# Softmax steps ahead of the weight split, and two gates behind the copy of turned probabilities

## The reference

```python
# first block, per layer
q = rmsnorm(d_q.reshape(b, s, DIFF_HEADS, 2, DIFF_HALF_DIM), diff_q_norm_g[l])
k = rmsnorm(d_k.reshape(b, s, DIFF_HEADS, 2, DIFF_HALF_DIM), diff_k_norm_g[l])
...
p = jax.nn.softmax(sc, axis=-1)                       # two maps for each head
o = einsum(p, v); o_d = o[:, :, 0] - lam * o[:, :, 1]
y_d = rmsnorm(o_d) * (1 - lam_init) * jax.nn.silu(d_g)
...
y_m = memory_attention(mq, mk, mv) * jax.nn.silu(m_g)
...
# second block: 16 heads, window 128, each with a sink in its softmax
m = jnp.maximum(jnp.max(s, axis=-1, keepdims=True), sink)
p = jnp.exp(s - m)
denom = jnp.sum(p, axis=-1, keepdims=True) + jnp.exp(sink - m)
```

## Time and profile before

| what | value |
|---|---|
| median of 3 runs | 2598.99 us |
| lowest, highest run | 2596.06, 2602.8 us |
| span of the profiled execution | 2596.0 us |
| PE busy | 2547.3 us (98% of the span) |
| PE weight loads busy | 2175.1 us (84%) |
| DVE busy | 1939.5 us (75%) |
| ACT busy | 1300.1 us (50%) |
| mean granted TensorE clock | 0.995 |
| DMA | 556.64 MB, mean 214 GB/s |

### The profile page before, as it was taken

How to read it: one execution, slowest core, us unless ns; L and a number is a source line. 1 busy time by engine, 2 the same in 40 slices (tenths; PEclk the granted TensorE clock), 3 DMA queues, 4 the chain that set the end, 5 groups by cost and what they waited for, 6 DMA issues and landing times.

```text
span 2596.0 us, 35319 instructions
## 1 busy us (share of the span) xinstructions
PE 2547.3 (98%) x13936; PEld 2175.1 (84%) x13936; DVE 1939.5 (75%) x2769; ACT 1300.1 (50%) x1758; POOL 10.8 (0%) x62
## 2 busy tenths in 40 slices
PE   7999999999999999999999999999999999999998
PEld 6888888888888887888788888888888888888886
DVE  6877766887777687676667787887788887788855
ACT  7544555554455555454444554544644443444443
POOL 0000000000000010000000000000000000000000
PEclk9999999999999999999999999999999999999999
DMA  8687554778754466755567788888476668976764
GB/s 271 219 299 244 160 154 143 228 258 286 242 158 152 149 214 218 235 171 154 153 190 222 231 277 277 270 282 272 143 197 189 188 208 307 284 203 196 201 194 140
DMA packets 526519, 556.64 MB, mean 214 GB/s; under 512 B 17409, under 2 KB 453762, under 8 KB 526226
## 3 DMA queue, kind: packets, MB, share of 16 engines
q1 hardware_dynamic: 526354, 554.38, 68.4%
HBM read 552.22 MB, written 2.10 MB: 214 GB/s over the span
## 4 chain that ended last, share of the span: by engine, by line
PE 88%; DVE 7%; ACT 3%; issue 1%; DMA 0%; DVEq 0%; SPq 0%; ACTq 0%
PE ACC L468 43%; PE ACC L473 21%; PE ACC L415 6%; PE ACC L417 6%; PE ACC L416 6%; DVE WL L549 2%; PE OU L1268 1%; ACT WH L540 1%; PE SC L1235 1%; PE SC L1247 1%; ACT PROB L1293 1%; PE SC L1276 1%; DVE XH L1138 0%; DVE XH L1146 0%; DVE PROB L1352 0%
## 5 line engine op out<-in xcount | busy, mean ns | idle before, releaser
L468 PE MATMUL ACC<-XH,WH 128*128 128x512 f32 x5296 | 1692.3, 401 | 21.2 <-DVE XH L1146 15.3
L540 ACT ACTIVATE WH<-RAW 128x1024 fp32r<-128x1024 f32 (+1 forms) x852 | 897.9, 1057 | 1166.5 <-PE ACC L473 836.1
L549 DVE TENSOR_TENSOR WL<-RAW,WH 128x1024 fp32r<-128x1024 f32 (+1 forms) x852 | 1032.6, 1220 | 568.5 <-ACT WH L540 567.0
L473 PEld LDWEIGHTS ACC<-XH,WL 128*128 128x128 f32 x5296 | 998.7, 189 | 236.6
L473 PE MATMUL ACC<-XH,WL 128*128 128x256 f32 x5296 | 1044.2, 279 | 0.0
L468 PEld LDWEIGHTS ACC<-XH,WH 128*128 128x128 f32 x5296 | 814.4, 189 | 41.2 <-issue 18.5
L1932 DVE SCALAR_TENSOR_TENSOR RAWMOD<-RAWMOD,CSILU 128x1024 f32<-128x1024 f32 x192 | 233.8, 1218 | 1.0 <-DMA RAWMOD<-in_w_mod_t 0.7
L415 PE MATMUL ACC<-WH,XH 128*128 128x512 f32 x384 | 151.9, 396 | 3.6 <-DVE WL L549 3.6
L416 PE MATMUL ACC<-WL,XH 128*128 128x512 f32 x384 | 149.6, 390 | 0.0
L417 PE MATMUL ACC<-WH,XH 128*128 128x512 f32 x384 | 149.5, 389 | 0.0
L415 PE MATMUL ACC<-WH,AH 128*128 128x512 f32 x352 | 137.3, 390 | 0.0
(11 more groups left out here) (287 smaller groups left out, 1438.0 us busy)
## 6 DMA issues: line engine op xcount, KB each, us to landing
RAW<-in_w_in SPq DMA_DIRECT2D x408, 512.0 KB, 4.5
RAWMOD<-in_w_mod_t SPq DMA_DIRECT2D x192, 512.0 KB, 4.9
RAW<-in_w_up SPq DMA_DIRECT2D x176, 512.0 KB, 4.7
RAW<-in_w_out SPq DMA_DIRECT2D x96, 512.0 KB, 5.4
RAW<-in_w_down SPq DMA_DIRECT2D x88, 512.0 KB, 5.0
RAW<-in_w_mem_kv SPq DMA_DIRECT2D x32, 512.0 KB, 5.8
RAW<-in_w_branch_gla SPq DMA_DIRECT2D x32, 512.0 KB, 5.1
RAW<-in_w_branch_attn SPq DMA_DIRECT2D x16, 512.0 KB, 5.2
```

The lines of the kernel that those rows point to most:

```text
L468: return pe.matmul(bank, k.WH[:, w % RING, kc, cols], x, start=tile == 0, stop=False)
L473: return pe.matmul(bank[:, 0:T], k.WL[:, w % RING, kc, cols], x[:, 0:T], start=False, stop=tile == tiles - 1)
L540: act.activation(k.WH[:, slot, :, 0:width], k.RAW[:, r % RAWS, :, 0:width], ACT.Copy).then_inc(k.hi_ready, 1)
L549: dve.tensor_tensor(k.WL[:, slot, :, 0:width], k.RAW[:, k.plan.unit_load[unit] % RAWS, :, 0:width], k.WH[:, slot, :, 0:width].bitcast(F32) ...
```

## The change

Nothing is added or removed; steps change place on ACT and DVE. Two new functions take the softmax steps out of `act_beside` and `dve_beside` and are called ahead of the split: `dve_softmax` (maxima and scaling) and `act_softmax` (exponentials). `dve_next_squares` at w = 7 is also called ahead of the split. In the first mem turn of each layer the two gates with their table loads go from w = 4 to w = 5, behind `act_copy_turned`.

```diff
@@ act_token_stage @@
+            act_softmax(act, k, stage, j, q)
             if not late:
                 token_split_ahead(act, k, stage, w, act_split)
@@ act_stage, turn @@
+                act_softmax(act, k, stage, i, b * stage.per_pair + q)
                 split_ahead(act, k, stage, i, b * stage.per_pair + q, last, act_split)
@@ dve_token_stage @@
+            dve_softmax(dve, k, stage, j, q, chain)
             if not late:
                 token_split_ahead(dve, k, stage, w, dve_split)
@@ dve_stage, turn @@
+                if w == 7:
+                    dve_next_squares(dve, k, stage, i, last)
+                dve_softmax(dve, k, stage, i, w, chain)
                 split_ahead(dve, k, stage, i, w, last, dve_split)
...
-                if w == 7:
-                    dve_next_squares(dve, k, stage, i, last)
@@ new @@
+def act_softmax(act, k, stage, i, w):
+
+    u, kind = unit_beside(stage, i), stage.beside
+    if u is not None and w == (4 if kind == "win" else 3):
+        act_exps(act, k, kind, u, sinks=2 * (stage.first + i) if kind == "win" else None)
@@ act_beside @@
-    elif w == 4 and kind == "mem" and i == 0:
-        act.wait_ge(k.evacuated, stage.pair0)
-        act_silu(act, k, M_G, MEM_T)
-        act_silu(act, k, D_G, DIFF_T)
-        act.preload_act_table_set("natural_log_exp_and_others")
-    elif w == (4 if kind == "win" else 3):
-        act_exps(act, k, kind, u, sinks=2 * (stage.first + i) if kind == "win" else None)
     elif w == (6 if kind == "win" else 5):
         act_copy_turned(act, k, kind, u)
+        if kind == "mem" and i == 0:
+            act.wait_ge(k.evacuated, stage.pair0)
+            act_silu(act, k, M_G, MEM_T)
+            act_silu(act, k, D_G, DIFF_T)
+            act.preload_act_table_set("natural_log_exp_and_others")
@@ new @@
+def dve_softmax(dve, k, stage, i, w, chain):
+
+    u, kind = unit_beside(stage, i), stage.beside
+    if u is None:
+        return
+    late = 1 if kind == "win" else 0
+    if w == 2 + late:
+        head = 2 * (stage.first + i) if kind == "win" else i + stage.first
+        dve_maxima(dve, k, kind, u, chain, head=head)
+    elif w == 3 + late:
+        dve_probs(dve, k, kind, u, chain, layer=stage.layer)
```

More of the change, by code:

```diff
@@ L1442, in dve_beside @@
         return
-    late = 1 if kind == "win" else 0
     if w == 0 and kind != "win":
@@ L1449, in dve_beside @@
         dve_rotate(dve, k, stage.first + i, chain)
[L1450 to L1454, removed]
     elif w == 4 and kind == "mem" and i == 1:
```

## The result

The changed kernel takes 2576.01 us (median of 4 runs, 2574.52 to 2579.59), the kernel before in the same measurement 2598.93 us (2596.06 to 2602.8). The ratio is 0.9912, 95% interval 0.9898 to 0.9926: 22.9 us faster. The forecast was 15.3 us faster, 2583.7 us, with a range down to 2578. In a second measurement, the same two kernels gave 2579.83 and 2597.88 us (ratio 0.9925, 0.9912 to 0.9937), which is 18 us. So part of the first figure does not repeat. Two things have to be found: what my sum missed, and what varies from run to run.

What follows compares the result with a forecast made beforehand. PE, busy 2547.3 of 2596.0 us, was taken as the bound. Terms 8.4 + 1.4 + 1.8 + 3.7 = 15.3 us off the span gave a forecast median of 2583.7 us, range 2578 to 2592.

Steps and rivals of the forecast that it cites:

- Gates, 8.4 us: First memory turn of each layer: with the copy ahead of the gates, PE's wait for TURNED goes whole, 2 x 4.20 us.
- Squares, 1.4 us: Squares ahead of a DVE split end 1.2 us earlier; PE regains 1.4 us over 4 places, between 1.2 and 2.1.
- Maxima, exponentials, scaling, 5.5 us: Softmax steps ahead of the split: PE's waits for scaling go, 1.8 us for 12 diff waits, 3.7 for 8 window waits.
- Displaced splits, 0 us: Splits moved behind softmax steps cost nothing; in the diff turn their cover shrinks from 7.3 to 4.1 us.
- Rival C: Splits behind the scaling in 24 units come late, so PE waits for weights; 2618 us, chance 0.04.
- A: Only the gates pay; in softmax units PE waits as long for something else; 2590.6 us, chance 0.11.
- D: Nothing is regained: the copy stays late or PE waits elsewhere; median near 2599 us, chance 0.05.
- B: Moved gates make the squares late in each layer, past 1.0 us of cover; 2586.9 or 2590.3 us, chance 0.08.

Runs made afterwards that it cites:

- e3_squares: Only the squares moved ahead of the split, against the kernel before: 2591.91 us against 2597.88, ratio 0.9972.
- e2_softmax: Only maxima, exponentials and scaling moved ahead of the split, against the kernel before: 2586.5 us against 2597.88, ratio 0.9961.

## Why the prediction was wrong in size

*Gates, 8.4 us.* The step was right: the copy went ahead, the wait went whole, w = 6 to w = 0 fell from 11.59 to 7.38 us, and the mean of that term over both layers is as forecast. It consists of 5.1 us that the two waits cost at full clock (2 x 2.53, by w = 6 in e3_squares) and 3.3 us of clock behind them. The kernel before paid the second part in each of its three profiles, but not every kernel with such a wait did. The 8.4 us thus rested partly on luck: had the clock not fallen in the profile at hand, the same reading would have given 5.1.

*Squares, 1.4 us: this is the step that failed most.* It measured 4.5. I counted the 4 places that the view of waits names and took its rows as both ends of the term, "between the ends 1.2 and 2.1". The squares came too late for the early weight load in 12 more places (0.19 or 0.12 us each, 2.1 in all). The 4 named ones cost 0.6 us and not 0.35. That is what the weight loads' own waits say (0.6 and 0.5 at the longest in the earlier trace rows); I had chosen a value near PE's idle time instead, which the view of waits of the kernel before has as

```profile
PE SC L1276 <- DVE SQ L1600: 0.7, 2, 0.4
PE SC L1276 <- DVE SQ L1604: 0.6, 2, 0.3
```

A comparison of whole units would have shown it: w = 0 takes 3.62 us in a diff turn, and nothing in it needs more than the 3.43 it takes now.

*Maxima, exponentials, scaling, 5.5 us.* They measured 6.8 (2.6 and 4.2, where I had 1.8 and 3.7). The mechanism came out as told, down to the split that hides beside the exponentials. The size was off for the same reason: 0.22 us in a diff place and not 0.15, 0.44 and 0.61 in a window place. In the diff places the weight loads' own waits (2.4 us in the earlier trace rows) were nearly the full price of 2.6; in the window places the price of 4.2 lies between what I took and their 4.9. I had discounted them for overlap by too much. My reason for going by them, that a matmul cannot start before its weights are there, holds in the form that no matmul in the trace of before starts ahead of its own weight load; some start before the record of that load ends, as at 258.36 above.

*Displaced splits, 0 us.* Right: 4.06 us of lead against the 4.1 worked out. Rival C had nothing to start from.

*The range.* The two missed amounts are 4.4 us and would have put the forecast at 2579.3. The range failed with them: its low end was built on 17.8 us as the most that the terms could give, and they gave 19.7, since the squares (4.5) and the diff waits (2.6) lie above the high ends that I had written for them (2.1 and 2.4). The first measurement lies 3.3 us below 2579.3, the second 0.5 above. What is left is the clock away from the moved steps: the three profiles of before lose 6.8, 10.2 and 6.8 us there (the table less 3.4 behind the gates), those of the changed kernel 3.4, 8.5 and 3.4. I took the spread of three runs of before as the noise of both kernels, and held the changed kernel's profile to the clock of the profile at hand. All the runs of the three measurements together say more than three profiles: 28 of before have a mean of 2598.9 us, 10 of the changed kernel 2577.5, a difference of 21.4 us with a 95% interval of some 1.9 us to each side. That is 1.7 us more than the 19.7, and the 19.7 lies within the interval. So it is not shown that the changed kernel loses less clock elsewhere, and the first figure of 22.9 us was in part luck. What decides between a fall of the clock and none behind a wait of one length stays open; no run here tells it.

*Rivals.* A is excluded by e2_softmax, D by every profile; B was not reached, with 0.7 us to spare where I had worked out 1.0; C had 4.06.

## What to carry to other kernels

Where an engine's queue is in order, ask of each step which wait stands behind it, and put the step with the longest chain ahead of a step that has slack: the split had 7 us of lead and the softmax chain had none. Count what PE loses by comparing the same unit with and without the neighbour's work, not by the view of waits alone, because a producer that is just in time can cost PE its early weight load (0.2 us a place here) and be named nowhere. Before comparing two spans, take out what each lost to the granted clock; here that made the three profiles of each of two kernels agree to 0.3 us, where the spans of one of them differed by 5.4.

## What the runs showed of the hardware

- A wait of 2.26 or 2.27 us on PE costs 2.5 us (w = 6 in e3_squares, 6.94 against 4.41) or 4.2 us (before). The difference is a stretch in which the granted clock is a mix of its two levels, 1.2 and 2.4 GHz, right behind the wait: 1.71 us in the earlier trace rows.
- The clock can also fall where PE is busy throughout. In the changed kernel's first profile, at kv_a, between 1065 and 1080 us:

```profile
1065.00:1080.00 15.00, 15.00 (x73) 12.74 (x73) 5.59 (x10) 3.32 (x4) 0.00 (x0) 0.89 0.46 136
```

  In the first profile of before, the same stretch (1080 to 1095 there) is at 1.00, in its second at 0.77. What stands there are sixteen matmuls with 16 rows of weights among the usual ones. Within their second half or right behind them the clock falls in nine of the ten profiles, in all but the first of before; that they are the cause was not tried.
- A switch of ACT's table takes 1.28 us, and the next instruction starts 0.01 to 0.02 us after its end.
